# A transfer that adds in place of VectorE's subtraction: the low parts of the down-projection weights in the first network of a two-block fp32 kernel

## The reference, cut to what matters

```python
h = h + memory_cross_attention(...)
u = jax.nn.relu(rms_norm(h, norm_mlp_g) @ mlp_w1)   # 512x1024 @ 1024x4096
h = h + (u * u) @ mlp_w2                            # 512x4096 @ 4096x1024
```

## Time and profile before

| | |
|---|---|
| Median of 3 runs | 2175.72 us (2175.52 to 2175.83) |
| Span of the profiled execution | 2174.4 us |
| PE busy | 2157.7 us, 99% |
| DVE busy | 1144.9 us, 53% |
| ACT busy | 904.4 us, 42% |
| POOL busy | 0.2 us |
| DMA queue of SP | 197.66 MB, 29.0% of the 16 engines' span |
| First network | about 452 to 798 us of the span |

### The profile page before, as it was taken

The page is one execution under the profiler, slowest core; times in us unless marked ns, Lnnn a source line. Parts: engine busy times, 40 slices in busy tenths (PEclk is TensorE's granted clock), DMA queues, the critical chain, the costliest instruction groups (busy, mean ns, idle before and its releaser), DMA issues.

```text
span 2174.4 us, 28238 instructions
## 1 busy us (share of the span) xinstructions
PE 2157.7 (99%) x11510; PEld 1777.1 (82%) x11510; DVE 1144.9 (53%) x1985; ACT 904.4 (42%) x1526; POOL 0.2 (0%) x4
## 2 busy tenths in 40 slices
PE   9999999999999999999999999999999999999999
PEld 7888988888888888888888878887777888888887
DVE  4754664453433454344357677647776455434345
ACT  6654545442322332222234465546666233222224
POOL 0000000000000000000000000000000000000000
PEclk9999999999999999999999999999999999999999
DMA  5121521133333223323223622321111333333321
GB/s 186 59 78 59 194 97 59 59 95 99 97 94 99 94 90 98 104 87 107 86 90 95 199 80 82 98 83 49 45 30 40 97 97 97 98 97 97 98 87 68
DMA packets 190194, 199.45 MB, mean 92 GB/s; under 512 B 7777, under 2 KB 185074, under 8 KB 189554
## 3 DMA queue, kind: packets, MB, share of 16 engines
q1 hardware_dynamic: 190066, 197.66, 29.0%
HBM read 188.73 MB, written 2.10 MB: 88 GB/s over the span
## 4 chain that ended last, share of the span: by engine, by line
PE 97%; DVE 1%; ACT 1%; issue 1%; DMA 0%; SPq 0%; DVEq 0%; ACTq 0%
PE lin L557 28%; PE lin L559 27%; PE lin L558 27%; PE turned L658 3%; PE score L753 3%; PE mix L767 2%; PE mix L1201 1%; PE mix L1040 1%; PE score L1020 1%; PE score L869 1%; PE score L1252 0%; PE mix L1260 0%; PE score L1004 0%; PE mix L777 0%; DMA raw<-in_w_in_dram 0%
## 5 line engine op out<-in xcount | busy, mean ns | idle before, releaser
L557 PE MATMUL lin<-xh,wh 128*128 128x512 f32 (+1 forms) x1478 | 581.4, 393 | 1.7 <-DVE wl L2120 1.2
L559 PE MATMUL lin<-xh,wl 128*128 128x512 f32 (+1 forms) x1478 | 568.7, 385 | 0.0
L558 PE MATMUL lin<-xl,wh 128*128 128x512 f32 (+1 forms) x1478 | 567.6, 384 | 0.0
L557 PE MATMUL lin<-ah,wh 128*128 128x512 f32 x1044 | 407.8, 391 | 0.5 <-DVE h L2173 0.5
L559 PE MATMUL lin<-ah,wl 128*128 128x512 f32 x1044 | 405.5, 388 | 0.0
L558 PE MATMUL lin<-al,wh 128*128 128x512 f32 x1044 | 405.4, 388 | 0.0
L2114 DVE TENSOR_TENSOR wl<-raw,wh 128x2048 fp32r<-128x2048 f32 x129 | 295.7, 2292 | 185.1 <-ACT wh L1365 185.1
L1365 ACT ACTIVATE wh<-raw 128x2048 fp32r<-128x2048 f32 x129 | 245.8, 1906 | 263.6 <-PE lin L559 263.6
L557 PEld LDWEIGHTS lin<-xh,wh 128*128 128x128 f32 x1478 | 277.9, 188 | 63.1 <-issue 9.9
L559 PEld LDWEIGHTS lin<-xh,wl 128*128 128x128 f32 x1478 | 277.7, 188 | 56.5
L558 PEld LDWEIGHTS lin<-xl,wh 128*128 128x128 f32 x1478 | 278.2, 188 | 52.4 <-issue 1.0
(11 more groups left out here) (349 smaller groups left out, 2120.8 us busy)
## 6 DMA issues: line engine op xcount, KB each, us to landing
raw<-in_ffn_w_dram SPq DMA_DIRECT2D x60, 1024.0 KB, 5.3
raw<-in_w_in_dram SPq DMA_DIRECT2D x38, 1024.0 KB, 5.3
raw<-in_mlp_w_dram SPq DMA_DIRECT2D x32, 1024.0 KB, 5.4
raw<-in_xattn_wkv_dram SPq DMA_DIRECT2D x8, 1024.0 KB, 5.5
raw<-in_w_out_dram SPq DMA_DIRECT2D x8, 1024.0 KB, 5.1
arena<-arena SPq DMA_DIRECT2D x104, 64.0 KB, 2.0
raw<-in_ffn_w_dram SPq DMA_DIRECT2D x8, 768.0 KB, 4.6
raw<-in_xattn_wq_dram SPq DMA_DIRECT2D x4, 1024.0 KB, 5.3
```

The source lines that it names most:

```text
L557: nc.tensor.matmul(o, w[0], x[0], start=first, stop=False)
L558: nc.tensor.matmul(o, w[0], x[1], start=False, stop=False)
L559: return nc.tensor.matmul(o, w[1], x[0], start=False, stop=last)
```

## The change

The low parts of the sixteen down panels of the first network (`DOWN`) are no longer made by VectorE. For these panels ACT, ahead of its high-part copy, writes the negated and rounded weights (which is the negated high part) into `wl`, in two halves of four row blocks each. GpSimd waits for each half and issues a transfer from the weights in device memory onto that half of `wl`, with addition: weight minus high part, the low part. VectorE's `conv` for such a panel only waits for both transfers and for the high part, and counts up `conv_done`.

```diff
+DOWN = [P0["mlp"] + 8 * r_ + 4 + j_ for r_ in range(4) for j_ in range(4)]
@@ build
+        neg_half, lo_in = [sem("neg_half0"), sem("neg_half1")], [sem("lo_in0"), sem("lo_in1")]
@@ new list for GpSimd
+        @block.gpsimd
+        def _(pool):
+            for n, p in enumerate(DOWN):
+                r, j = divmod(n, 4)
+                for half in range(2):
+                    ks = slice(half * KT // 2, (half + 1) * KT // 2)
+                    pool.wait_ge(neg_half[half], n + 1)
+                    pool.dma_start(wl[:, p % 2, ks], mw2[:, r * KT:(r + 1) * KT, j * PC:(j + 1) * PC][:, ks], accum_op=ALU.add).then_inc(lo_in[p % 2], 16)
@@ ScalarE, conv(p)
                 if p >= 3:
                     act.wait_ge(lin_done, p * 2 - 2)
+                if p in DOWN:
+                    for half in range(2):
+                        ks = slice(half * KT // 2, (half + 1) * KT // 2)
+                        nc.scalar.activation(wl[:, p % 2, ks], raw[:, p % 2, ks], ACT.Copy, scale=-1.0).then_inc(neg_half[half], 1)
                 nc.scalar.activation(wh[:, p % 2], raw[:, p % 2], ACT.Copy).then_inc(hi_done, 1)
@@ VectorE, conv(p)
+                if p in DOWN:
+                    dve.wait_ge(lo_in[p % 2], 32 * (DOWN.index(p) // 2 + 1))
+                    dve.wait_ge(hi_done, whole(p) + 1)
+                    dve.sem_inc(conv_done, 1)
+                    return
                 dve.wait_ge(hi_done, whole(p) + 1)
                 nc.vector.tensor_tensor(wl[:, p % 2], raw[:, p % 2], wh[:, p % 2].bitcast(F32), ALU.subtract).then_inc(conv_done, 1)
```

## The result

The changed kernel takes 2213.84 us (median of 4 runs, 2212.36 to 2217.03), the kernel before 2175.77 us: a ratio of 1.0176, 95% interval 1.0164 to 1.0188. It is 38 us slower. The forecast was 2264 us, 88 us slower, with a range from 2177 to 2385: the sign and the place were right, the size was 2.3 times too large. The profiled execution has a span of 2210.5 us, 36.1 us above that of before.

The account below looks back on a forecast made before the run. The prediction took TensorE's own pace as the bound; late transfers at 12.3 us a panel pair add 16 L - 108.5 = 88 us to the 2174.4 us span, giving 2262, or 2264 us as run median; range 2177 to 2385.

Parts of the forecast that it names:

- TensorE's pace is the bound, and DVE's and ACT's relief or load are worth nothing: First network: PE busy 345.79 of 346.00 us; 36.7 us off DVE and 33.7 us more on ACT change nothing.
- The place and the chain: At 16 down panels, DVE's in-order wait for the transfers delays the read-out behind it, and so PE's next panel.
- The limits, 6.6 us of L for D0, 5.1 for D1, 5.7 and 5.0 in the last round: Transfer time each down panel can hide; PE loses the excess; 5.7 is last-round D2, 5.0 last-round D3.
- L: Time from the end of ACT's first negated half to the landing of both transfers of a down panel.
- L = 12.3 us, from three streams at the load's rate: Each pair of transfers reads, reads back and writes: 1.8 + 3 x 3.5 us, giving 88 us for the kernel.
- rival 2: Streams overlap in the down panels' transfers: two streams for each MB, 8.8 us, 32 us slower, 2208 us; chance 0.20.
- sum on record: Predicted PE loss over the 16 down panels, each by its own limit: 16 L - 108.5, 88 us at 12.3.
- D2 and D3 lose L - 8.5: Down panels D2 and D3, rounds 0 to 2 (6 panels): transfers free up to 8.5 us, any excess lost.
- The load beside the transfers: A whole load of `raw` between a down panel's transfers would make them 15.8 us: 144 us slower, 2320 us.
- The clock costs nothing: PE's clock falling in the gaps ahead of down panels adds nothing, with 44 us as the end.
- The restart, 1.0 us from landing to first matmul: After each landing: 0.69 us read-out, about 0.3 us for two handovers and the first weight load.
- The estimate by a page: GpSimd transfers by the skill's rule: 2.1 MB at 436 GB/s, 4.8 + 2.0 = 6.8 us; 11 us for the kernel.

Follow-up runs that it names:

- two pairs of runs: Low parts in separate buffers, early GpSimd transfers without subtraction against the kernel before with subtraction: 2180.59 against 2181.07 us; buffers at a multiple of 512 bytes, 2178.94 against 2179.58.

## Why the prediction was off, point by point

- *TensorE's pace is the bound, and DVE's and ACT's relief or load are worth nothing.* Right. Subtractions off DVE: at most 0.6 us in two pairs of runs. Copies on ACT: none.
- *The place and the chain: landing, DVE's wait, the read-out behind it, PE.* Right. It showed in the waits of after and in the run with the wait moved, which took back 19 of 38 us.
- *The limits, 6.6 us of L for D0, 5.1 for D1, 5.7 and 5.0 in the last round.* Right. With the second round's L of 9.0 and 8.8 they give 2.4 and 3.7 us; measured 2.2 and 3.75. In the last round L is 8.7 and 8.8, which gives 3.0 and 3.8; measured 3.1 and 3.7.
- *L = 12.3 us, from three streams at the load's rate.* This is the step that failed: the right term, mis-sized, and it carries nearly all of the error (16 times 3.3 us is 53 us). L is 9.0 with nothing beside it. Reading back and adding together bring the rate to a bit over half (177 against 318 GB/s) and cost 2.6 us a panel, so the bound "two streams", 8.8 us, was the nearest; it stood as rival 2, with 32 us. The sum on record at L = 9.0 gives 35.5 us, against 36.1 measured between the two spans. The agreement is in part luck: it leaves out the collisions, which add, and the next point, which takes off.
- *D2 and D3 lose L - 8.5.* Wrong as a rule. Their negated copies wait for the end of the panel two before, not for the start of the one before; a gap between the two is time that the transfers have for nothing. The loss is L - 8.5 less the gap ahead of the panel before. For D2: 11.8 - 8.5 - 2.0 = 1.3, measured 1.2; for D3: 10.9 - 8.5 - 1.1 = 1.3, measured 1.3. In round 0, where the gap ahead of D1 is 3.5 us, D2 loses 12.5 - 8.5 - 3.5 = 0.5; measured 0.4. At L = 12.3 the rule would have counted 3.8 us too much for D2 in each of three rounds, 11 of the 88 us.
- *The load beside the transfers.* Named as an end of the range and left out of the sum; in rounds 0 to 2 L is 0.9 to 3.5 us above 9.0 for D2 and D3, and between 8.7 and 9.1 when these loads are left out.
- *The clock costs nothing.* The reason given, that the next start hangs on the landing, holds for D0 in after, and for D2 of the last round (13.8 us long, hidden by D3's landing). That a gap of 3.8 us is too short to matter does not: behind a gap of 2.2 us the granted clock fell to 0.50, the lower of the two levels, and D0 took 12.6 us instead of 10.9. The Trainium skill's page "TensorE: Matmul & The Clock Gate", Part 1: The HAM clock gate, names these two states, and the trace agrees. The run without the colliding loads shows that the cost is only hidden: take the later wait away, and 1.7 us a round come out elsewhere.
- *The restart, 1.0 us from landing to first matmul.* Right (585.08 to 586.04, and 1.0 for the three panels after).
- *The estimate by a page.* The rule cited from the Trainium skill ("DMA: Bandwidth & Descriptors", Anatomy of one DMA — SWDGE (gpsimd) path) gave 6.8 us for the pair's bytes; the measured landing is 8.7 us after the first issue, and 5.7 for a lone half. The plain pair of the run without addition took 6.1 us from first issue to last landing. So the measurement decides against that estimate for adding transfers.

What stays open is why low parts in another buffer slow the matmuls by 3%; alignment is a part of it at most. Nor was it tried what sets whether the clock falls behind a given gap.

## What to carry to other kernels

Work taken off an engine that isn't the bound pays nothing, and work that replaces it pays the length of its chain as soon as that exceeds one step of the bound: compare the new chain, end to end, with the step, and count what stands behind the wait in the waiting engine's list, which here was half of the loss. As measured here, with rows of 1 KB, price a transfer that adds at half the data rate of a plain one, and give it a buffer that lets it start a step earlier. When several late steps follow each other, work out each from the event its start really waits for; a gap in one step is cover for the next.

## What was not expected of the hardware

An adding transfer of 512 KB from GpSimd takes 5.7 us alone and 5.6 as the first of a pair; a plain one, first of a pair, takes 3.8. Its row on POOL is 1.3 to 1.65 us long in the second round of after, though the next issue begins 0.9 us after it. The granted clock fell to 0.50 behind gaps of 2.0 to 2.2 us ahead of D0 in three rounds of after, and stayed at 1.00 in round 0 behind gaps of 2.1 us (ahead of D0) and 3.5 us (ahead of D1). And matmuls with 512 columns whose weights come by turns from two buffers begin 0.227 us apart or 0.233, by where one of the two buffers lies: 5 us over sixteen panels, 3.8 with the buffer at a multiple of 512 bytes.
